# Depthwise convolution taps in one stage of a decoder trunk: from TensorE to ScalarE and GpSimd, with 18 plain fp32 taps left for the last two tiles

## What is computed

```python
def conformer_conv_module(h, w_in, b_in, w_dw, b_dw, ln_g, ln_b, w_out, b_out):
    u = h @ w_in + b_in
    a, gate = jnp.split(u, 2, axis=-1)
    u = a * jax.nn.sigmoid(gate)
    u = lax.conv_general_dilated(
        u, w_dw[:, None, :], window_strides=(1,), padding=[(CONV_WIDTH - 1, 0)],
        dimension_numbers=("NWC", "WIO", "NWC"), feature_group_count=D_MODEL) + b_dw
    u = jax.nn.silu(layer_norm(u, ln_g, ln_b))
    return u @ w_out + b_out
```

## Time and profile before

| | us |
|---|---|
| median of 3 runs | 2216.06 (2214.51 to 2217.22) |
| profiled execution, its own time | 2215.75 |
| its span | 2214.0 |
| PE busy | 2192.6 (99%), 13136 matmuls |
| DVE busy | 1417.3 (64%) |
| ACT busy | 1006.6 (45%) |
| POOL busy | 208.1 (9%), nearly all in the first 236 us |
| convolution stage | about 14 to 237 |

### The profile page before, as it was taken

The page is one execution under the profiler, slowest core; times in us unless marked ns, Lnnn a source line. Parts: engine busy times, 40 slices in busy tenths (PEclk is TensorE's granted clock), DMA queues, the critical chain, the costliest instruction groups (busy, mean ns, idle before and its releaser), DMA issues.

```text
span 2214.0 us, 32918 instructions
## 1 busy us (share of the span) xinstructions
PE 2192.6 (99%) x13136; PEld 1945.1 (88%) x13136; DVE 1417.3 (64%) x1319; ACT 1006.6 (45%) x890; POOL 208.1 (9%) x125
## 2 busy tenths in 40 slices
PE   8999899999999999999999999999999999999998
PEld 8999788888888888888888898888888888888887
DVE  7999877555555554556767667775565556555655
ACT  7665645443344433444444444444443344433444
POOL 7999100000000000000000000000000000000000
PEclk9999999999999999999999999999999999999999
DMA  9665354546554555455454435555555554555462
GB/s 238 169 175 166 117 207 171 209 171 209 189 190 171 208 189 196 171 209 190 172 172 142 143 115 204 186 204 175 202 173 206 175 204 174 206 190 190 172 212 77
DMA packets 250048, 400.54 MB, mean 181 GB/s; under 512 B 6407, under 2 KB 72143, under 8 KB 249935
## 3 DMA queue, kind: packets, MB, share of 16 engines
q1 hardware_dynamic: 249406, 398.74, 53.3%
q0 software_dynamic: 352, 0.56, 0.1%
q10 hardware_dynamic: 208, 0.07, 0.0%
HBM read 397.24 MB, written 2.10 MB: 180 GB/s over the span
## 4 chain that ended last, share of the span: by engine, by line
PE 89%; DVE 6%; issue 2%; DVEq 1%; DMA 0%; POOL 0%; ACT 0%; SPq 0%; ACTq 0%; POOLq 0%
PE bank L1317 54%; PE bank L1319 28%; DVE bank L980 4%; PE bank L1618 4%; PE bank L1603 1%; PE bank L1680 1%; PE bank L1414 0%; DVEq L979 0%; DMA x_rows<-in_x 0%; DVE bank L991 0%; DVE u L961 0%; DVE bank L988 0%; DVE act L942 0%; PE bank L1417 0%; PE bank L1550 0%
## 5 line engine op out<-in xcount | busy, mean ns | idle before, releaser
L1317 PE MATMUL bank<-x_both,w_hi 128*128 128x512 f32 x3328 | 1155.9, 393 | 0.0
L843 DVE TENSOR_TENSOR w_lo<-raw,w_hi 128x2048 fp32r<-128x2048 f32 x343 | 779.0, 2289 | 528.3 <-ACT w_hi L529 528.1
L529 ACT ACTIVATE w_hi<-raw 128x2048 fp32r<-128x2048 f32 x374 | 707.6, 1910 | 627.7 <-PE bank L1319 601.1
L1319 PE MATMUL bank<-x_both,w_lo 128*128 128x256 f32 x3328 | 927.0, 279 | 0.0
L1317 PEld LDWEIGHTS bank<-x_both,w_hi 128*128 128x128 f32 x3328 | 623.3, 187 | 141.4 <-issue 0.3
L1317 PE MATMUL bank<-h_both,w_hi 128*128 128x512 f32 x1872 | 651.1, 393 | 0.4 <-DVE h_both L1026 0.4
L1319 PEld LDWEIGHTS bank<-x_both,w_lo 128*128 128x128 f32 x3328 | 627.0, 188 | 0.1
L1319 PE MATMUL bank<-h_both,w_lo 128*128 128x256 f32 x1872 | 521.6, 279 | 0.0
L1317 PEld LDWEIGHTS bank<-h_both,w_hi 128*128 128x128 f32 x1872 | 350.8, 187 | 81.0 <-issue 0.5
L1319 PEld LDWEIGHTS bank<-h_both,w_lo 128*128 128x128 f32 x1872 | 352.6, 188 | 0.0
L1400 PE MATMUL bank<-x_both,w_hi 128*128 128x256 f32 x960 | 173.5, 283 | 0.0
(11 more groups left out here) (230 smaller groups left out, 1271.7 us busy)
## 6 DMA issues: line engine op xcount, KB each, us to landing
raw<-in_ffn_w_gate_up SPq DMA_DIRECT2D x176, 1024.0 KB, 4.9
raw<-in_ffn_w_down SPq DMA_DIRECT2D x88, 1024.0 KB, 5.1
raw<-in_gla_w_in SPq DMA_DIRECT2D x48, 1024.0 KB, 5.2
raw<-in_conv_w_in SPq DMA_DIRECT2D x32, 1024.0 KB, 6.0
raw<-in_conv_w_out SPq DMA_DIRECT2D x16, 1024.0 KB, 5.1
raw<-in_gla_w_out SPq DMA_DIRECT2D x16, 1024.0 KB, 6.6
x_rows<-in_x SPq DMA_DIRECT2D x4, 512.0 KB, 6.4
out<-out_rows SPq DMA_DIRECT2D x4, 512.0 KB, 3.1
```

The source lines that it names most:

```text
L529: nc.scalar.activation(w_hi[k][:, :, :], raw[k][:, :, :], ACT.Copy).then_inc(hi_done, 1)
L843: nc.vector.tensor_tensor(w_lo[k][:, :, :], raw[k][:, :, :], w_hi[k][:, :, :].bitcast(F32), ALU.subtract).then_inc(lo_done, 1)
L1317: mm(to, w_hi[k][:, kt, cols], xx[:, :, k0 + kt, :], start=(first and kt == 0), stop=False, skip_group_check=True)
L1319: ins = mm(to[:, 0:T], w_lo[k][:, kt, cols], xx[:, 0, k0 + kt, :], start=False, stop=(last and kt == 3), skip_group_check=True)
```

## The change

`PE_TAPS` goes. In every tile ScalarE makes six tap products: one with the bias `b_dw` added (`tap_first`), four into `tap_four`, one into `tap_last`. GpSimd adds the four in one pass of 512 columns (`add_four`: 4 x 256 to 2 x 256) and no longer makes `u_lo` or `tap_sum`. VectorE keeps 25 taps in the first fourteen tiles; its first step now reads `tap_first` instead of the bias, its second reads the SBUF tensor `shift` instead of PSUM, steps 13 and 14 add the halves of `tap_four`, step 15 adds `tap_last`. The last but one step writes its sum to `act`, so one join is left in place of two. `u` of the next tile (`gated`) is made after step 16 instead of at the start of a tile. `u_hi`, `u_lo`, `dw_hi`, `dw_lo`, `y_pe` and the diagonals of each tile are gone. In tiles 14 and 15 TensorE does 4 and 14 taps, as plain fp32 matmuls with diagonals that ScalarE makes in tiles 5 and 7, after all products, and VectorE adds them from PSUM (`join_last`). Squares of tiles 0 to 7 are made early, in the last turn, into a buffer of their own; GpSimd adds twice, and TensorE sums the four left.

```diff
-PE_TAPS = 2
-ACT_TAPS = 4
-MORE_TAPS = (2, 10)
-DVE_TAPS = TAPS - PE_TAPS - ACT_TAPS
-TAP_STEPS = DVE_TAPS + 2
-ALL_TAPS = KT * TAP_STEPS - sum(MORE_TAPS)
-JOIN_AT = 6
-UW = T + PE_TAPS + MORE_TAPS[1]
+ACT_TAPS = 6
+LAST_TAPS = (4, 14)
+DVE_TAPS = TAPS - ACT_TAPS
+TAP_STEPS = DVE_TAPS + 3
+ALL_STEPS = KT * TAP_STEPS - sum(LAST_TAPS)
+JOIN_AT = 4
+ADD_AT = 13
+NEXT_U_AT = 16
...
+            def add_four(tile):
+
+                pool.wait_ge(product_done, ACT_TAPS * tile + 5)
+                nc.gpsimd.tensor_tensor(tap_four[:, 0:2, :], tap_four[:, 0:2, :], tap_four[:, 2:4, :], ALU.add).then_inc(four_added, 1)
...
                     lo(4 * i + (4 + j), j % RING)
                     sum_y(2 * i + t)
                     if not (last and t == 1):
                         lo(4 * i + (5 + j), (j + 1) % RING)
-                    split_u(2 * i + (2 + t), t)
-                    sum_pair(2 * i + (2 + t))
+                    add_four(2 * i + (2 + t))
...
+                    product(0, tap_first[:, :], ACT.Identity, bias=vec[:, ds(VCOL["conv_b_dw"] + tile, 1)])
+                    for n in range(4):
+                        product(1 + n, tap_four[:, n, :], ACT.Copy)
+                    product(5, tap_last[:, :], ACT.Copy)
...
+                    if n == 0:
+                        dve.wait_ge(product_done, ACT_TAPS * tile + 1)
+                        nc.vector.scalar_tensor_tensor(out=acc, in0=tap, scalar=w, in1=tap_first[:, :],
+                                                       op0=ALU.mult, op1=ALU.add).then_inc(tap_done, 1)
                     elif n == 1 and shifted:
-                        dve.wait_ge(shift_done, 1)
-                        nc.vector.scalar_tensor_tensor(out=acc, in0=u[:, t, j:j + T], scalar=w, in1=shift_bank[t],
+                        dve.wait_ge(shift_kept, 1)
+                        nc.vector.scalar_tensor_tensor(out=acc, in0=tap, scalar=w, in1=shift[:, :],
                                                        op0=ALU.mult, op1=ALU.add).then_inc(tap_done, 1)
...
+            def last_taps(n):
+
+                pe.wait_ge(acc_read[n], U_CONV_IN // 2 + KT // 2)
+                for j in range(LAST_TAPS[n]):
+                    at = n * LAST_TAPS[0] + j
+                    pe.wait_ge(diag_done, at + 1)
+                    ins = mm(y_last[n], last_diag[at][:, :], u[:, n, j:j + T], start=(j == 0), stop=(j == LAST_TAPS[n] - 1))
                 ins.then_inc(pe_taps, 1)
...
+            with pe.Fori(2, KT // 2) as i:
+                for t in range(2):
+                    conv_product(i, t)
+            last_taps(0)
+            last_taps(1)
```

More of the change, by code:

```diff
@@ L138, in trunk @@
         gate = sb("gate", [P, 2, T], 67 * K)
[L139 to L157, removed]
+        tap_first = sb("tap_first", [P, T], 70 * K)
+        tap_last = sb("tap_last", [P, T], 71 * K)
+        tap_four = sb("tap_four", [P, 4, T], 192 * K)
+        sq_early = sb("sq_early", [P, 8, T], 72 * K)
+        last_diag = [sb(f"last_diag{j}", [P, P], 80 * K + 512 * j) for j in range(sum(LAST_TAPS))]
+        assert sum(LAST_TAPS) <= 18
         y_sum = sb("y_sum", [P, T], 69 * K)
-        ln_sq = sb("ln_sq", [P, KT, T], 32 * K)
+        sq_late = sb("sq_late", [P, 8, T], 32 * K)
         shift_w = sb("shift_w", [P, P], small + 5696)
@@ L604, in _ @@
             hi(0, 2)
[L607 to L620, removed]
             def conv_turn(i, last=False):
@@ L956, in conv_tile @@
                 if not first:
[L957 to L960 removed]
+                    dve.wait_ge(tap_done, TAP_STEPS * (tile - 1))
                 nc.vector.scalar_tensor_tensor(out=u[:, t, PAD:PAD + T], in0=slot[t][:, 0, :],
@@ L963, in conv_tile @@
                                                in1=gate[:, t, :], op0=ALU.add, op1=ALU.mult).then_inc(acc_read[t], 1)
+            def conv_tile(i, t, on_pe=0, fewer=0, shifted=True, add_at=ADD_AT, last=False):
+                tile = 2 * i + t
+                done = TAP_STEPS * t - fewer + 2 * TAP_STEPS * i
+                first = isinstance(i, int) and i == 0
+                if not first:
+                    dve.wait_ge(join_done, tile - 1)
                 dve.wait_ge(acc_read[t], U_CONV_IN // 2 + i + 1)
-                for n, j in enumerate(range(PE_TAPS + more, TAPS - ACT_TAPS)):
+                j = on_pe
+                for n in range(TAP_STEPS - on_pe):
@@ L981, in conv_tile @@
                                                        op0=ALU.mult, op1=ALU.add).then_inc(tap_done, 1)
-                    if join_at <= n < join_at + 2 and not (first and t == 0):
-                        join(tile - 1, 1 - t, n - join_at)
-                n = DVE_TAPS - more
-                acc = y_acc[t][:, n % 2, :]
-                dve.wait_ge(pair_sum, tile + 1)
-                dve.wait_ge(tap_done, done + (n - 1))
-                nc.vector.tensor_tensor(acc, acc, tap_sum[:, :], ALU.add).then_inc(tap_done, 1)
@@ L989, in conv_tile @@
-                dve.wait_ge(pair_done, 2 * tile + 2)
-                dve.wait_ge(tap_done, done + (n + 1))
-                nc.vector.tensor_tensor(y_acc[t], y_acc[t], tap_pair[1][:, :, :], ALU.add).then_inc(tap_done, 1)
+                        j += 1
+                    if n == JOIN_AT and not (first and t == 0):
+                        join(tile - 1, 1 - t)
+                    if n == NEXT_U_AT and not last:
+                        gated(i + t, 1 - t)
+                    if n == JOIN_AT + 4 and last:
+                        join_last(0)
@@ L993, in _ @@
+            gated(0, 0)
             for i in range(2):
@@ L998, in _ @@
                     conv_tile(i, t)
-            conv_tile(KT // 2 - 1, 0, MORE_TAPS[0])
-            conv_tile(KT // 2 - 1, 1, MORE_TAPS[1], fewer=MORE_TAPS[0], join_at=JOIN_AT + 4)
-            dve.wait_ge(tap_done, ALL_TAPS)
-            for part in range(2):
-                join(KT - 1, 1, part)
+            conv_tile(KT // 2 - 1, 0, LAST_TAPS[0])
+            conv_tile(KT // 2 - 1, 1, LAST_TAPS[1], fewer=LAST_TAPS[0], add_at=9, last=True)
+            dve.wait_ge(tap_done, ALL_STEPS)
+            join(KT - 1, 1)
+            join_last(1)
             dve.wait_ge(stat_done, STAT[1] - 1)
```

224 lines of the change are left out of this document (72 added, 152 removed).

## The result

The changed kernel takes 2231.26 us (median of 4 runs, 2229.03 to 2232.75) against 2215.28 us for the kernel before on the same chip (4 runs, 2214.26 to 2217.22): a ratio of 1.007, 95% interval 1.0053 to 1.0088. It is slower by 0.7%. The profiled execution took 2231.23 us (span 2229.5), so it stands for the median.

A forecast was written before the change was run, and what follows sets the result against it. VectorE was taken to set the convolution stage's end, with TensorE full afterwards. 2215.75 - 16.8 = 2199.0 us without waits, plus 42.6 of VectorE waiting behind GpSimd, gave 2241.6, some 2242; range 2197 to 2254.

The forecast's parts named there:

- The likeliest case: VectorE steps 0 and 1, both inputs in SBUF, wait for whole GpSimd `w_lo` passes: 2230 to 2254 us, chance 0.61.
- The rivals without a wait or with mere slowing: VectorE beside GpSimd: no interference, 2197.5 to 2201 us, chance 0.29; or steps only slowed, 11 us, 2210, chance 0.05.
- The sum without waits: Convolution stage with no interference: variance at 219.7 instead of 236.47, 16.8 us sooner, so 2199.0 us.
- how often it hits: Tiles 4 to 15: 8 full `w_lo` waits of 4.58 us, 36.6, plus 6 us of small ones, 42.6 in all.
- Few hits: Rival: step 1 mostly gets the port right behind step 0; only some five passes are waited for, 2214 us, chance 0.05.
- When the pass starts: GpSimd can start the tile's `w_lo` pass 4.9 to 5.1 us after `u`, together with VectorE's steps 0 and 1.
- TensorE in the stage: TensorE waits about 4 us in a tile, then runs at 1.2 GHz; a product becomes some 13.3 us, hidden within 16.2.
- The 18 plain taps: Plain fp32 matmuls at the stage's end, 0.43 us each, 7.8 us on TensorE, hidden while VectorE works on the last tile.
- The early row: L1010 in the old trace, two SBUF inputs beside GpSimd's L504: 0.46 us against 0.408 to 0.419 for L1018, taken as waiting.

The follow-up runs named there:

- half passes: Changed kernel with each GpSimd `w_lo` pass written as two of half the columns; 2219.97 us, ratio 1.0021 to the kernel before.

## Why the prediction was right, point by point

- **The direction and the cause.** Forecast 2242 with a range of 2197 to 2254; measured 2231.26. The range held a faster and a slower outcome at once (0.34 against 0.61), so that the time lies in it says little; the mechanism is what was tested. The likeliest case, a wait for a whole pass, is what happened, and its own range (2230 to 2254) holds the time, near its lower end. The rivals without a wait or with mere slowing fell: the longest step took 4.87 us, and 0.39 us of shift moved 14.6 us.
- **The sum without waits, 2199.0.** The kernel with both tensors in PSUM gives 2199.74. Last join 217.62 (forecast 217.3), last `u` 207.88 (207.2), periods 11.51 and 11.79 us in turn in the later tiles, 11.65 in the mean (11.62), end of the products about 206.3 (206.2). The variance came at 220.63, 0.9 us later than the 219.7 forecast; 0.6 of that is the way from the last join, 3.0 us where the sum had 2.4. This half of the sum was sound.
- **The step that was mis-sized: how often it hits.** I took 8 full waits of 4.58 us, 36.6, and 6 us of small ones: 42.6. There were 5 full waits of about 4.35 (21.8 us) and 10.6 us in smaller ones, together 32.4. So the sum had 15 us too much for the full waits and 5 us too little for the small ones, and the two errors offset each other in part. The size of one was right within 0.25 us, since the earlier trace rows had the pass; the count was too high. Two things failed. I let a tile in which VectorE wins push GpSimd late, so that the next step 0 must wait; but in tiles 10 to 13 GpSimd itself waited 0.2 to 0.9 us for ScalarE's `w_hi` ahead of that pass (the three rows above), so nothing was handed on. And I had the return of the loop at 0.14 us, as in the old loop, but it took 0.27 in the new one: 5.10 against 5.37 us after `u`, with the pass at 5.21. I used it as a small addition, where it decides which tiles lose. "At least every second of the 12 tiles" was one too many: five of twelve were full waits, tiles 10, 12 and 14 among them. "Some five passes" is what the rival *Few hits* said, at 0.05; its sum added only two of them (2214). With five it is 2199 + 6 + 5 x 4.6 = 2228, closer to the measured time than my 2242.
- **When the pass starts.** Forecast 4.9 to 5.1 us after `u`, measured 5.21: in the loop the first product starts 0.73 us after `u` (181.72 - 180.99), not the 0.52 of the earlier trace rows (I had allowed 0.2 more, not surely), and the six products with `w_hi` took 4.4 us where I had 4.3. It is a tenth of a microsecond, in a contest where the starts lay 0.1 to 0.2 us apart.
- **TensorE in the stage.** Forecast: it waits about 4 us in a hit tile and its clock falls, hidden. It waited for `w_lo` six times, at most 4.5 us, with granted clocks of 0.86 and 0.80 in the 25 us stretches above; the waits on VectorE (32.4) already account for all but 1.0 us of the span. So it was hidden.
- **The 18 plain taps.** Forecast 0.43 us each and hidden. With both tensors in PSUM the 14 of the last tile took 6.31 us, 0.45 each, and ended at 214.7, ahead of the last joins (217.09 and 217.62). In the changed kernel they ended at 244.9, ahead of 248.15. They are not always: with `u` one step later they ended behind VectorE, as told above. I had about 8 us for them beside 11 on VectorE, lower clock included; there they took 9.30 us from 216.36 on, and VectorE was through with its own steps at 224.64.
- **The early row.** L1010's excess of 0.05 us was worth leaning on. In the kernel after, with GpSimd idle by then, the same operation (L952) took 0.42 instead of 0.46, as L1018 did. The Trainium skill ("SBUF — State Buffer", section "Who interferes with whom") says that a VectorE instruction with two SBUF inputs contends with a GpSimd instruction that reads SBUF, that the one that issues second is fully blocked, and that one with at most one SBUF input, outside some performance modes, doesn't contend. The traces agree in the main: 4.83 us at 170.23, 5.16 us for GpSimd at 188.65, and 0.489 us as the most of 334 taps. The recorded starts don't always tell who comes second, as tile 4 of the changed kernel shows.

## What to carry to other kernels

Before a VectorE operand is moved from PSUM to SBUF, look at what GpSimd does at that moment: two SBUF inputs beside a GpSimd pass can cost as long as that pass, here 4.83 us for an operation of 0.48. The page shows it as busy time, so look at the least and the most of a line, not at idle time, and where two queues meet within 0.3 us, expect the outcome of each loop iteration to hang on things like the loop's return. Keep one of the inputs in PSUM; where that isn't possible, shorter GpSimd instructions shorten the wait (32.4 to 21.9 us here), and so does moving the operation away from the pass (to 9.3).

## What the runs showed of the hardware that I had not expected

- A full wait can span more than one GpSimd instruction. With `tap_first` in PSUM, step 1 of tile 4 started in the middle of the sum of four and got in only after the pass behind it, which ended at 90.07:

```profile
84.77 5.59 DVE L910 SCALAR_TENSOR_TENSOR bank<-u,dw,shift 128x256 f32<-128x256 f32 x1
```

```profile
84.19 1.30 POOL L421 TENSOR_TENSOR tap_four<-tap_four 128x512 f32<-128x512 f32 x1
85.44 4.63 POOL L375 TENSOR_TENSOR w_lo<-raw,w_hi 128x2048 fp32r<-128x2048 f32 x1
```

  With the half passes the waiting step got in between the two halves. So who follows at the border of two instructions isn't fixed; the runs don't show by what.
- The other way round GpSimd pays too: 5.16 and 5.20 us for a pass of 4.6 when two VectorE steps in a row went ahead of it, and in the changed kernel 5.08 us in tile 4.
- Some kernels with such waits spread more: 2197.86 to 2200.83 (4 runs) with both tensors in PSUM, but 2210.8 to 2222.45 (10 runs) with `u` one step later. The changed kernel doesn't: 2229.03 to 2232.75 (4 runs). That the spread comes from contests lost and won is my reading; only one execution of each was looked at in its trace.
